# Layer two of a two-layer decoder on one Trainium2 core: gate and up products by Strassen's seven, results through DRAM, down projection chunk by chunk

## The chip, the cores and the metric

The kernel runs on one core of one Trainium2 chip. Its engines work side by side and meet at semaphores: TensorE (PE; its weight loads are PEld), VectorE (DVE), ScalarE (ACT), GpSimd (POOL), and SyncE (SP), whose queue issues all DMAs of the part in question. The metric is the device time in microseconds (us) from start to end of one execution; lower is better.

## The reference, cut to what matters

A decoder trunk on x of 1024 tokens by D = 1024: a convolution layer with a gated feed-forward, then a differential-attention layer with another, then a final RMSNorm. Only the second feed-forward changes:

```
def rmsnorm(x, g):
    x32 = x.astype(jnp.float32)
    y = x32 * lax.rsqrt(jnp.mean(x32 * x32, axis=-1, keepdims=True) + EPS)
    return (y * g.astype(jnp.float32)).astype(x.dtype)
...
def swiglu(h, w1, w3, w2):
    return (jax.nn.silu(h @ w1) * (h @ w3)) @ w2
...
        x = x + swiglu(rmsnorm(x, ffn_norm_g[layer]), ffn_w1[layer], ffn_w3[layer], ffn_w2[layer])
...
    return rmsnorm(x, final_norm_g)
```

All tensors are float32, D_FF = 2816.

## The kernel before, in words

**Numbers.** A float32 product is made of three matmuls: each operand is split into a high part of type fp32r (a copy by ACT, which rounds) and a low part (operand minus high part, by DVE), and PE adds low weight by high data, high weight by low data, high by high (`product`). Names end in h and l for the two parts: `Wh`, `Wl` for weights, `Sh`, `Sl` for the normed input with features on partitions.

**Sizes.** P = 128, KC = D / P = 8 pieces of the contraction, FC = 2816 / 128 = 22 chunks of hidden features, HT = 512 tokens in a half; the halves are LA and LB. A block of weights is 128 x 1024 float32 (512 KB). `load` brings it into one of two buffers `raw` (rows of 512 bytes), ACT's `hi` and DVE's `lo` split it into one of RING = 4 slots, and `raw` is loaded again after `lo` of the block two earlier (`load` waits for `w_lo`).

**Layer two's feed-forward** is the object `F1`. Its 22 chunks come in groups of 6, 6, 6 and 4. For each chunk of a group, a w1 block and a w3 block are multiplied with both halves (`both`, 2 x 24 matmuls of 512 columns a block); DVE scales the results by `rstd` (L1307, L1316), ACT takes the silu, DVE multiplies (L1319) and splits (L1281) them into `G1h`, `G1l` in SBUF. After each of the first three groups, KC blocks of w2 are multiplied with the group's chunks and DVE adds the results to the residual `xT` (L1326). The weight of the last group's w2 (`Th`, `Tl`, `TAIL_SIZE` = 4 chunks) serves three parts of the tokens, `PARTS`, of 512, 256 and 256 tokens. In the last parts PE also turns finished token blocks back (`y_chunks`, 8 transposes of 128 x 128 at L1605 for a block of 128 tokens), ACT sums their squares (L1102), DVE scales (`y_row`, L1590) and SP stores them.

**Order.** All orders are written out by hand, an engine runs its list in order, and a wait holds up everything behind it on its engine.

## Time and profile before

| | |
|---|---|
| median of 3 timed runs | 2398.87 us (2397.82 to 2400.33) |
| the profiled execution, its own time | 2400.49 us |
| its span, first to last instruction | 2398.7 us |
| PE busy | 2340.0 us (98%) |
| DVE busy | 1404.3 us (59%) |
| ACT busy | 800.7 us (33%) |
| mean granted TensorE clock, share of full speed | 0.994 |
| moved by DMA | 154.63 MB, mean 64 GB/s |

The profiled execution's own time lies 1.8 us over its span, and 1.6 us over the median. Matmuls overlap in the profile: the busy time of one is longer than the distance from its start to the next start, so what PE costs is read from distances between starts.

### The profile page before, as it was taken

How to read it: one execution, taken by the hardware profiler on the slowest of the kernel's cores; microseconds unless marked ns; L12 is line 12 of the kernel's file. 1: busy time of each engine (PE TensorE's matmuls, PEld its weight loads, DVE VectorE, ACT ScalarE, POOL GpSimd, SP SyncE). 2: the span in 40 equal slices, each digit the busy share in tenths (PEclk: the TensorE clock that was granted, in tenths of full speed). 3: DMA queues.
4: the chain of work that ended last, by engine and by line, in shares of the span. 5: the costliest groups of instructions: out<-in, count | busy, mean ns of one | idle time of the engine just before them, and what ended most of it. 6: DMA issues, size and time to landing. Idle time of an engine off the chain costs nothing.

```text
span 2398.7 us, 27168 instructions
## 1 busy us (share of the span) xinstructions
PE 2340.0 (98%) x10989; PEld 1899.4 (79%) x10989; DVE 1404.3 (59%) x2145; ACT 800.7 (33%) x1381; POOL 68.2 (3%) x51
## 2 busy tenths in 40 slices
PE   7999989999999999999999999899999999999998
PEld 6875868888788888887777777677888888888888
DVE  6996599999456544446677767656532332233334
ACT  5312432222344322224555555644321111121112
POOL 0000000000000000002111111000000000000000
PEclk9999999999999999999999999999999999999999
DMA  4110323333233333331011111111112111111112
GB/s 137 44 37 17 86 73 96 98 89 96 82 100 92 105 88 97 98 97 52 19 36 49 42 44 48 62 41 36 53 36 62 44 55 51 53 42 46 53 45 80
DMA packets 278010, 154.63 MB, mean 64 GB/s; under 512 B 5669, under 2 KB 273278, under 8 KB 277886
## 3 DMA queue, kind: packets, MB, share of 16 engines
q1 hardware_dynamic: 277886, 152.90, 21.7%
q8 instruction: 88, 1.44, 0.3%
q14 instruction: 36, 0.29, 0.0%
HBM read 145.54 MB, written 7.34 MB: 64 GB/s over the span
## 4 chain that ended last, share of the span: by engine, by line
PE 89%; DVE 7%; ACT 2%; issue 1%; SPq 0%; DMA 0%; DVEq 0%; ACTq 0%
PE ps L1773 28%; PE ps L1622 19%; PE ps L1624 18%; PE ps L1623 18%; PE ps L1605 3%; DVE cacc L1190 2%; DVE cvA L1190 1%; PE ps L1725 1%; DVE sc L1436 1%; ACT sc L964 1%; PE ps L1687 1%; DVE Wl L1115 0%; PE ps L1677 0%; DVE Sl L1351 0%; DVE Wl L1391 0%
## 5 line engine op out<-in xcount | busy, mean ns | idle before, releaser
L1622 PE MATMUL ps<-Sh,Wl 128*128 128x512 f32 x1616 | 656.9, 406 | 20.7 <-DVE Sl L1273 7.4
L1624 PE MATMUL ps<-Sh,Wh 128*128 128x512 f32 x1616 | 632.9, 392 | 0.0
L1623 PE MATMUL ps<-Sl,Wh 128*128 128x512 f32 x1616 | 632.2, 391 | 0.0
L1622 PEld LDWEIGHTS ps<-Sh,Wl 128*128 128x128 f32 x1616 | 305.5, 189 | 99.2 <-issue 27.8
L1624 PEld LDWEIGHTS ps<-Sh,Wh 128*128 128x128 f32 x1616 | 304.7, 189 | 65.8
L1115 DVE TENSOR_TENSOR Wl<-raw,Wh 128x1024 fp32r<-128x1024 f32 (+2 forms) x238 | 280.3, 1178 | 125.2 <-ACT Wh L750 123.5
L1623 PEld LDWEIGHTS ps<-Sl,Wh 128*128 128x128 f32 x1616 | 305.5, 189 | 60.2 <-issue 3.8
L750 ACT ACTIVATE Wh<-raw 128x1024 fp32r<-128x1024 f32 (+2 forms) x238 | 240.8, 1015 | 294.5 <-DMA raw<-in_ffn_w_dram 137.3
L1773 PE MATMUL ps<-Sh,Wl 128*128 128x512 f32 x688 | 213.3, 391 | 2.5 <-DVE Sl L1351 2.4
L1773 PE MATMUL ps<-Sl,Wh 128*128 128x512 f32 x688 | 212.4, 390 | 0.0
L1773 PE MATMUL ps<-Sh,Wh 128*128 128x512 f32 x688 | 212.3, 390 | 0.0
L1326 DVE TENSOR_TENSOR xT<-ps,xT 128x512 f32<-128x512 f32 x96 | 64.0, 688 | 214.7 <-PE ps L1773 133.6
L1773 PEld LDWEIGHTS ps<-Sh,Wl 128*128 128x128 f32 x688 | 129.5, 188 | 30.6 <-issue 3.3
L1773 PEld LDWEIGHTS ps<-Sl,Wh 128*128 128x128 f32 x688 | 129.7, 188 | 26.9
L1773 PEld LDWEIGHTS ps<-Sh,Wh 128*128 128x128 f32 x688 | 129.5, 188 | 27.0
L1316 DVE TENSOR_TENSOR tmp<-ps,rstd 128x512 f32<-128x512 f32 x66 | 45.4, 689 | 167.3 <-PE ps L1773 130.6
L1622 PE MATMUL ps<-G0h,Wl 128*128 128x512 f32 x352 | 138.6, 394 | 0.0
L1624 PE MATMUL ps<-G0h,Wh 128*128 128x512 f32 x352 | 137.0, 389 | 0.0
L1623 PE MATMUL ps<-G0l,Wh 128*128 128x512 f32 x352 | 137.0, 389 | 0.0
L874 ACT ACTIVATE tmp<-tmp 128x512 f32<-128x512 f32 x66 | 41.0, 632 | 262.1 <-DVE tmp L1307 262.1
L1307 DVE TENSOR_TENSOR tmp<-ps,rstd 128x512 f32<-128x512 f32 x66 | 43.5, 687 | 139.7 <-PE ps L1773 116.5
L977 ACT ACTIVATE ATh<-ps 128x512 fp32r<-128x512 f32 (+2 forms) x96 | 47.0, 490 | 202.3 <-PE ps L1605 202.3
(196 smaller groups left out, 3116.5 us busy)
## 6 DMA issues: line engine op xcount, KB each, us to landing
raw<-in_ffn_w_dram SPq DMA_DIRECT2D x148, 512.0 KB, 3.8
raw<-in_pw_w_dram SPq DMA_DIRECT2D x32, 512.0 KB, 3.8
raw<-in_ffn_w_dram SPq DMA_DIRECT2D x32, 448.0 KB, 3.7
raw<-in_ffn_w_dram SPq DMA_DIRECT2D x24, 384.0 KB, 3.4
xrow<-in_x_dram SPq DMA_DIRECT2D x8, 512.0 KB, 6.6
raw<-in_w_q_dram SPq DMA_DIRECT2D x8, 512.0 KB, 4.7
raw<-in_w_k_dram SPq DMA_DIRECT2D x8, 512.0 KB, 4.1
raw<-in_w_v_dram SPq DMA_DIRECT2D x8, 512.0 KB, 3.9
```

What stands on the lines that cost most here:

```text
L750: act.activation(flat(ring_hi(b)), flat(raw[b % 2][:, 0:n, :]), ACT.Copy).then_inc(w_hi, 1)
L977: act.activation(ATh[:, j0:j0 + nj, (i % 2) * P:(i % 2 + 1) * P], ps[:, BANK[key], 0:nj * P].rearrange("p (j q) -> p j q", q=P), ACT.Copy) ...
L1115: dve.tensor_tensor(flat(ring_lo(b)), flat(raw[b % 2][:, 0:n, :]), flat(ring_hi(b)).bitcast(F32), ALU.subtract).then_inc(w_lo, 1)
L1190: dve.scalar_tensor_tensor(dst, src, wj, dst, ALU.mult, ALU.add).then_inc(conv_s, 1)
L1307: dve.tensor_tensor(plain, ps[:, bank, :], rstd[:, hf, :], ALU.mult).then_inc(t1_ok, 1)
L1316: dve.tensor_tensor(gated, ps[:, bank, :], rstd[:, hf, :], ALU.mult).then_inc(t3_ok, 1)
L1326: dve.tensor_tensor(X(c, hf), by_block(ps[:, bank, :]), X(c, hf), ALU.add).then_inc(add_ok, 1)
L1605: return pe.transpose(dst, src, ident[0:m, 0:m])
L1622: pe.matmul(dst, ll, rh, start=start, stop=False)
L1623: pe.matmul(dst, lh, rl, start=False, stop=False)
L1624: return pe.matmul(dst, lh, rh, start=False, stop=stop)
L1773: ins = pe.matmul(ps[:, banks[j], :], (Wh if m else Wl)[s][:, k, :], l if m == 1 else h, start=k == 0 and m == 0, stop=k == chunks - 1 and ...
```

## The change

`F1` keeps one group of four chunks (CHUNKS0), without w2. The other 18 chunks go in pairs; for each pair there is one *unit* for w1 (u even) and one for w3 (u odd), UNITS = 18. A unit takes two chunks by two halves of tokens by two halves of the contraction (HC = 4 pieces) as a 2 x 2 by 2 x 2 product of quarters, in Strassen's way (Winograd's form): PE makes seven products of 4 x 3 matmuls (A11, S2, A12, S1, S3, S4, A22) in place of eight. DVE makes four sums of weight quarters a unit (`weight_sums_first`, `weight_sums_last`), splits seven (`up_low`), and combines the seven results by seven additions from PSUM (`read`), four scalings and, for odd units, four multiplications. The sums of input quarters (T1 to T4) are made once, beside the plain group. `raw[0]` and `raw[1]` hold the two chunks of one unit, and `up_load(u)` fills both after the last `up_low` of the unit before. Products go round through all eight banks of PSUM.

The 44 hidden tiles (22 chunks, 2 halves) are stored to `g_dram`. The down projection takes 22 chunks for each of the three parts, 66 *steps*: a step loads one chunk of w2 for all 1024 outputs (512 KB, rows of 4096 bytes) and the chunk's hidden tile, both are split, and PE adds 8 x 3 matmuls into eight results that stay in PSUM over all 22 steps. So w2 is loaded three times. Turns of finished blocks (`Y_TURN_AT`) follow steps 2, 6, 10 and 14 of part 1 and steps 4 and 9 of part 2; the last two blocks' turns follow the last step.

```
-F1 = Ffn(1, (LA, LB), (6, 6, 6, 4), WO0 + KC + 1, F0B.result0 + F0B.results(), 2 * FC, FC, 6 * KC, False, True)
-
+F1 = Ffn(1, (LA, LB), (4,), WO0 + KC + 1, F0B.result0 + F0B.results(), 2 * FC, FC, 6 * KC, False, True)
...
+CHUNKS0 = F1.sizes[0]
+UNITS = FC - CHUNKS0
+PRODUCTS = 7
+ALL_PRODUCTS = PRODUCTS * UNITS
+USLOTS = 8
+HC = KC // 2
+A11, S2, A12, S1, S3, S4, A22 = range(PRODUCTS)
...
+UBANKS = (6, 7, 4, 5, 0, 1, 2, 3)
...
+DOWN_ORDER = ((2, 3, 6, 7, 4, 5, 0, 1), tuple(range(KC)), tuple(range(KC)))
+DOWN_BANK = (tuple((n, 0) for n in range(KC)), tuple(((2, 3, 6, 7)[n // 2], n % 2 * HT // 2) for n in range(KC)),
+             tuple(((4, 5, 0, 1)[n // 2], n % 2 * HT // 2) for n in range(KC)))
+STEPS_D = len(PARTS) * FC
...
+Y_TURN_AT = {(1, 2): 0, (1, 6): 1, (1, 10): 2, (1, 14): 3, (2, 4): 4, (2, 9): 5}
...
+            def up_load(u):
+                if u:
+                    sp.wait_ge(u_lo, PRODUCTS * u)
+                else:
+                    sp.wait_ge(w_lo, TAIL)
+                for r in range(2):
+                    sp.dma_start(raw[r][:, :, :], cols(up3 if u % 2 else up1, CHUNKS0 + 2 * (u // 2) + r)) \
+                        .then_inc(u_in[r], 16)
...
+            def unit_store(u, j):
+                sp.wait_ge(u_g, 4 * (u // 2) + j + 1)
+                c, hf = tiles(u)[j]
+                sp.dma_start(g_dram[c, hf], st[:, j, :]).then_inc(g_out[j], 16)
+            def down_load(d):
+                if d >= 2:
+                    sp.wait_ge(dw_lo, d - 1)
+                else:
+                    sp.wait_ge(u_lo, ALL_PRODUCTS)
+                sp.dma_start(raw[d % 2][:, :, :], down[d % FC]).then_inc(dw_in[d % 2], 16)
+            def hidden_load(d):
+                if d >= 4:
+                    sp.wait_ge(dg_lo, d - 3)
+                else:
+                    sp.wait_ge(up_mm, ALL_PRODUCTS - PRODUCTS + S2 + 1)
...
+                sp.dma_start(graw[d % 4][:, 0:w], g_dram[k, hf, :, c0:c0 + w]).then_inc(dg_in[d % 4], 16)
...
+            def second_layer():
+                blocks = list(F1.order())
+                for _, what, c, b in blocks[0:4]:
+                    load(b, cols(up1 if what == "w1" else up3, c))
+                for i in range(len(blocks)):
+                    if i + 4 < len(blocks):
+                        _, what, c, b = blocks[i + 4]
+                        load(b, cols(up1 if what == "w1" else up3, c))
+                    if i == 6:
+                        up_load(0)
+                    if i % 2:
+                        hidden_store(i // 2)
+                for u in range(UNITS):
+                    if u + 1 < UNITS:
+                        up_load(u + 1)
+                    else:
+                        down_load(0)
+                        down_load(1)
+                    if u % 2:
+                        for j in range(4):
+                            unit_store(u, j)
+                            if u == UNITS - 1 and j < 2:
+                                hidden_load(2 * j)
+                                hidden_load(2 * j + 1)
+                for j in range(4):
+                    sp.wait_ge(g_out[j], 16 * (UNITS // 2))
+                sp.dma_start(grow[:, :], a["final_norm_g"].unsqueeze(0).broadcast_to([P, D])).then_inc(grow_in, 16)
+                for d in range(2, STEPS_D):
+                    down_load(d)
+                    if d >= 4:
+                        hidden_load(d)
+                    t = y_behind(d - 8)
+                    if t is not None:
+                        y_store(t)
...
+            def up_high(u, j):
+                q = PRODUCTS * u + j
+                if j == A11:
+                    for r in range(2):
+                        act.wait_ge(u_in[r], 16 * (u + 1))
+                if j in (S1, S2, S3, S4):
+                    act.wait_ge(u_sum, 4 * u + (S1, S2, S3, S4).index(j) + 1)
+                if q >= USLOTS:
+                    act.wait_ge(up_mm, q - USLOTS + 1)
+                else:
+                    act.wait_ge(mm, results_through(TAIL - RING + q // 2))
...
+                act.activation(flat(Uh[uslot(q)]), flat(src), ACT.Copy).then_inc(u_hi, 1)
...
+            for u in range(UNITS):
+                act.wait_ge(up_mm, PRODUCTS * u + 1)
+                if u:
+                    act.wait_ge(u_ev, READS * (u - 1) + E_11)
+                else:
+                    act.wait_ge(g_st[LA], 16 * CHUNKS0)
+                act.activation(p1, ps[:, ubank(PRODUCTS * u + A11), :], ACT.Copy).then_inc(p1_ok, 1)
+                for turn, js in enumerate(((A11,), (S2, A12, S1), (S3, S4), (A22,), ())):
+                    if u + 1 < UNITS:
+                        for j in js:
+                            up_high(u + 1, j)
+                    if u % 2 == 0 and turn < 4:
+                        up_silu(u, turn)
...
+            for d in range(STEPS_D):
+                act.wait_ge(dw_in[d % 2], 16 * (d // 2 + 1))
+                if d < RING:
+                    act.wait_ge(up_mm, ALL_PRODUCTS - USLOTS + 2 * d + 2)
+                else:
+                    step_done(act, d - RING)
+                act.activation(flat(Wh[down_slot(d)]), flat(raw[d % 2]), ACT.Copy).then_inc(dw_hi, 1)
...
+                act.activation(Dh[d % 4][:, 0:w], graw[d % 4][:, 0:w], ACT.Copy).then_inc(dg_hi, 1)
+                t = y_behind(d - 3)
+                if t is not None:
+                    y_square(t)
...
+            def up_low(u, j):
...
+                dve.wait_ge(u_hi, q + 1)
+                dve.tensor_tensor(flat(Ul[r]), flat(src), flat(Uh[r]).bitcast(F32), ALU.subtract).then_inc(u_lo, 1)
...
+            def weight_sums_first(u):
+                for r in range(2):
+                    dve.wait_ge(u_in[r], 16 * (u + 1))
+                s1 = up_slot(u, S1)
+                dve.tensor_tensor(s1, raw[1][:, 0:HC, :], raw[1][:, HC:KC, :], ALU.add).then_inc(u_sum, 1)
+                dve.wait_ge(u_sum, 4 * u + 1)
+                dve.tensor_tensor(s2v[:, :, :], s1, raw[0][:, 0:HC, :], ALU.subtract).then_inc(u_sum, 1)
+            def weight_sums_last(u):
+                s3 = up_slot(u, S3)
+                dve.tensor_tensor(s3, raw[0][:, 0:HC, :], raw[1][:, 0:HC, :], ALU.subtract).then_inc(u_sum, 1)
+                dve.wait_ge(u_sum, 4 * u + 2)
+                s4 = up_slot(u, S4)
+                dve.tensor_tensor(s4, raw[0][:, HC:KC, :], s2v[:, :, :], ALU.subtract).then_inc(u_sum, 1)
...
+            def read(u, j, reads, to, other):
+                dve.wait_ge(up_mm, PRODUCTS * u + j + 1)
+                dve.tensor_tensor(to, ps[:, ubank(PRODUCTS * u + j), :], other, ALU.add).then_inc(u_ev, 1)
+                dve.wait_ge(u_ev, READS * u + reads)
+            def result_of(u, i, j, reads, other, hf):
+                c0 = u // 2
+                to = va if u % 2 else st[:, i, :]
+                if u % 2 == 0 and c0:
+                    dve.wait_ge(g_out[i], 16 * c0)
+                elif u % 2 and 4 * c0 + i:
+                    dve.wait_ge(u_g, 4 * c0 + i)
+                read(u, j, reads, to, other)
+                dve.tensor_tensor(to, to, rstd[:, hf, :], ALU.mult).then_inc(u_t, 1)
+                if u % 2:
+                    dve.wait_ge(u_t, 4 * u + i + 1)
+                    dve.wait_ge(u_silu, 4 * c0 + i + 1)
+                    dve.tensor_tensor(st[:, i, :], to, st[:, i, :], ALU.mult).then_inc(u_g, 1)
+            ffn(F1, beside_f1)
+            sum_low(0, 3)
+            up_low(0, A22)
+            dve.wait_ge(t_lo, 4 * HC)
+            for hf in F1.halves:
+                dve.wait_ge(g_st[hf], 16 * CHUNKS0)
+            for u in range(UNITS):
+                more = u + 1 < UNITS
+                dve.wait_ge(p1_ok, u + 1)
+                read(u, S2, E_Q6, q6, p1)
+                result_of(u, 0, A12, E_11, p1, LA)
+                if more:
+                    weight_sums_first(u + 1)
+                    up_low(u + 1, A11)
+                read(u, S1, E_U4, u4, q6)
+                if more:
+                    up_low(u + 1, S2)
+                    up_low(u + 1, A12)
+                    up_low(u + 1, S1)
+                result_of(u, 1, S3, E_22, u4, LB)
+                read(u, S3, E_U3, q6, q6)
+                if more:
+                    weight_sums_last(u + 1)
+                result_of(u, 2, S4, E_12, u4, LB)
+                if more:
+                    up_low(u + 1, S3)
+                    up_low(u + 1, S4)
+                result_of(u, 3, A22, E_21, q6, LA)
+                if more:
+                    up_low(u + 1, A22)
...
+            for d in range(STEPS_D):
+                dve.wait_ge(dw_hi, d + 1)
+                dve.tensor_tensor(flat(Wl[down_slot(d)]), flat(raw[d % 2]), flat(Wh[down_slot(d)]).bitcast(F32),
+                                  ALU.subtract).then_inc(dw_lo, 1)
+                w = PARTS[d // FC][1]
+                dve.wait_ge(dg_hi, d + 1)
+                dve.tensor_tensor(Dl[d % 4][:, 0:w], graw[d % 4][:, 0:w], Dh[d % 4][:, 0:w].bitcast(F32),
+                                  ALU.subtract).then_inc(dg_lo, 1)
+                if d % FC == 2 and d > FC:
+                    down_adds(d // FC - 1)
+                t = y_behind(d - 3)
+                if t is not None:
+                    if t == 0:
+                        dve.wait_ge(grow_in, 16)
+                    y_row(t)
...
+            def product_read(q):
+                u, j = q // PRODUCTS, q % PRODUCTS
+                if j == A11:
+                    pe.wait_ge(p1_ok, u + 1)
+                else:
+                    pe.wait_ge(u_ev, READS * u + last_read[j])
+            def up_product(u, j):
+                q = PRODUCTS * u + j
+                pe.wait_ge(u_lo, q + 1)
+                if u == 0 and j in sums_of:
+                    pe.wait_ge(t_lo, HC * sums_of[j])
+                if q >= len(UBANKS):
+                    product_read(q - len(UBANKS))
...
+                h, l = quarters[j]
+                r = uslot(q)
+                for k in range(HC):
+                    ins = product(ps[:, ubank(q), :], Uh[r][:, k, :], Ul[r][:, k, :], h[:, k, :], l[:, k, :], k == 0,
+                                  k == HC - 1)
+                ins.then_inc(up_mm, 1)
+            for u in range(UNITS):
+                for j in range(PRODUCTS):
+                    up_product(u, j)
...
+            for d in range(STEPS_D):
+                part, k = d // FC, d % FC
+                w = PARTS[part][1]
+                pe.wait_ge(dw_lo, d + 1)
+                pe.wait_ge(dg_lo, d + 1)
+                r = down_slot(d)
+                for n in DOWN_ORDER[part]:
+                    bank, c0 = DOWN_BANK[part][n]
+                    if k == 0:
+                        down_free(part, n)
+                    ins = product(ps[:, bank, c0:c0 + w], Wh[r][:, n, :], Wl[r][:, n, :], Dh[d % 4][:, 0:w],
+                                  Dl[d % 4][:, 0:w], k == 0 and c0 == 0, k == FC - 1 and c0 + w == HT)
+                    if k == FC - 1:
+                        ins.then_inc(d_res, 1)
+                if k < FC - 1:
+                    ins.then_inc(d_step, 1)
+                t = y_behind(d)
+                if t is not None:
+                    y_chunks(t, range(KC))```

**PE, in a unit.** The rows are matmuls (moving and stationary operand named; `Uh`, `Ul` are the slots of weight quarters, T3 the input sum for S3). Before, a w1 block:

```order
L1773 MATMUL ps<-Sh,Wl_111 128x512 [waits add_ok,w_lo]
```

Of the change, the first row of five products that follow one another, without the eleven of each between them:

```order
L1979 MATMUL ps<-T3h,Ul_94 128x512 [waits u_ev,u_lo]
...
L1979 MATMUL ps<-Sh,Ul_95 128x512 [waits u_ev,u_lo]
...
L1979 MATMUL ps<-T4h,Ul_96 128x512 [waits u_ev,u_lo]
...
L1979 MATMUL ps<-Sh,Ul_89 128x512 [waits u_ev,u_lo]
...
L1979 MATMUL ps<-T2h,Ul_90 128x512 [waits p1_ok,u_lo]
```

A block waited once for 48 matmuls; a product waits for 12, for its weight quarter (`u_lo`) and for its bank (`u_ev`, `p1_ok`).

**DVE, from a w1 unit into a w3 unit.** Before, a w1 and a w3 block had this list (two results scaled, a block's low part, two results scaled and multiplied, the hidden low parts):

```order
L1307 TENSOR_TENSOR tmp_73<-ps,rstd 128x512 [waits mm] x2
L1115 TENSOR_TENSOR Wl_110<-raw_104,Wh_106 128x1024 [waits w_hi]
L1316 TENSOR_TENSOR tmp_73<-ps,rstd 128x512 [waits mm]
L1319 TENSOR_TENSOR tmp_73<-tmp_73 128x512 [waits silu_ok,t3_ok]
L1316 TENSOR_TENSOR tmp_73<-ps,rstd 128x512 [waits mm]
L1319 TENSOR_TENSOR tmp_73<-tmp_73 128x512 [waits silu_ok,t3_ok]
L1281 TENSOR_TENSOR G1l<-tmp_73,G1h 128x512 [waits hid_hi] x2
```

Now, from the last `up_low` of one unit to the sums and low parts of the next:

```order
L1827 TENSOR_TENSOR Ul_96<-raw_139,Uh_88 128x512 [waits u_hi]
L1873 TENSOR_TENSOR q_107<-ps,p_106 128x512 [waits up_mm,p1_ok]
L1873 TENSOR_TENSOR va<-ps,p_106 128x512 [waits up_mm,u_ev]
L1885 TENSOR_TENSOR va<-va,rstd 128x512 [waits u_ev]
L1889 TENSOR_TENSOR st<-va,st 128x512 [waits u_silu,u_t]
L1842 TENSOR_TENSOR Us_100<-raw_139 128x512 [waits up_mm,u_in1,u_in0]
L1844 TENSOR_TENSOR s2v<-Us_100,raw_138 128x512 [waits u_sum]
L1827 TENSOR_TENSOR Ul_89<-raw_138,Uh_81 128x512 [waits u_hi]
L1873 TENSOR_TENSOR u_108<-ps,q_107 128x512 [waits up_mm]
L1827 TENSOR_TENSOR Ul_90<-s2v,Uh_82 128x512 [waits u_hi,u_ev]
L1827 TENSOR_TENSOR Ul_91<-raw_138,Uh_83 128x512 [waits u_hi]
L1827 TENSOR_TENSOR Ul_92<-Us_100,Uh_84 128x512 [waits u_hi]
```

Between the first row, which frees `raw` (its last reader), and L1842, which waits for both new chunks (`u_in0`, `u_in1`), stand four operations of w3 units and three of w1 units; the rest of the unit stands behind L1842.

**SP, in units and in steps.** Before, each load waited for the low part two blocks earlier:

```order
L565 DMA raw_104<-in_ffn_w_dram 128x8x128 [waits w_lo]
L565 DMA raw_105<-in_ffn_w_dram 128x6x128 [waits w_lo]
```

Now two units, with the four stores of a w3 unit, and further on two steps of part 1:

```order
L681 DMA raw_138<-in_ffn_w_dram 128x8x128 [waits u_lo]
L681 DMA raw_139<-in_ffn_w_dram 128x8x128
L693 DMA g_dram<-st 128x512 [waits u_g] x4
L681 DMA raw_138<-in_ffn_w_dram 128x8x128 [waits u_lo]
L681 DMA raw_139<-in_ffn_w_dram 128x8x128
...
L700 DMA raw_139<-in_ffn_w_dram 128x1024 [waits dw_lo]
L714 DMA graw_114<-g_dram 128x256 [waits g_out1,dg_lo]
L700 DMA raw_138<-in_ffn_w_dram 128x1024 [waits dw_lo]
L714 DMA graw_111<-g_dram 128x256 [waits g_out2,dg_lo]
```

Both chunks of a unit are now asked for at once, behind the stores where there are any, and every step has a second load behind that of w2.

## Rows read from the trace of the kernel before

**Rows 1.** The page: span, and busy time of the engines.

```profile
span 2398.7 us, 27168 instructions
PE 2340.0 (98%) x10989; PEld 1899.4 (79%) x10989; DVE 1404.3 (59%) x2145; ACT 800.7 (33%) x1381; POOL 68.2 (3%) x51
```

**Rows 2.** Busy time by stretch: layer two's feed-forward; its columns first.

```profile
core 0: us, PE busy (x) PEld busy (x) DVE busy (x) ACT busy (x) POOL busy (x), PEclk, DMA share, GB/s
1661.00:2339.00 678.00, 677.90 (x2979) 560.26 (x2979) 244.31 (x322) 137.68 (x191) 0.00 (x0) 1.00 0.17 49
```

**Rows 3.** The chain that ended last: start, us, engine, line, count.

```profile
1686.45 642.06 PE ps L1773 x2832
```

**Rows 4.** Timeline of PE in the tail: start, us, engine, line, operation.

```profile
2361.10 0.28 PE L1623 MATMUL ps<-G1l,Th 128*128 128x256 f32 x1
...
2362.30 0.28 PE L1624 MATMUL ps<-G1h,Th 128*128 128x256 f32 x1
2362.42 1.04 PE L1605 MATMUL ps<-ident,xT 128*128 128x128 f32 x8
2363.22 0.36 PE L1622 MATMUL ps<-G1h,Tl 128*128 128x256 f32 x1
```

**Rows 5.** Timeline of DVE: operations of 512 columns, chained and unchained.

```profile
1655.26 3.85 DVE L1477 TENSOR_TENSOR xT<-ps,xT 128x512 f32<-128x512 f32 x6
...
1659.90 10.69 DVE L1351 SCALAR_TENSOR_TENSOR Sl<-xT,vec,Sh 128x512 fp32r<-128x512 f32 x16 [0.79 <-ACT Sh L1089]
...
1708.17 0.69 DVE L1316 TENSOR_TENSOR tmp<-ps,rstd 128x512 f32<-128x512 f32 x1 [1.46 <-PE ps L1773]
1708.89 0.69 DVE L1319 TENSOR_TENSOR tmp<-tmp 128x512 f32<-128x512 f32 x1
1709.50 0.68 DVE L1316 TENSOR_TENSOR tmp<-ps,rstd 128x512 f32<-128x512 f32 x1
```

**Rows 6.** Tile raw from 1661 to 2300 us: min/median/max ns, then landing.

```profile
L750 ACT ACTIVATE Wh<-raw x65: 828/1043/1061, 1669.0 to 2299.0; 128x1024 fp32r<-128x1024 f32 x41, 128x768 fp32r<-128x768 f32 x24
L1115 DVE TENSOR_TENSOR Wl<-raw,Wh x64: 948/1216/1226, 1670.5 to 2287.7; 128x1024 fp32r<-128x1024 f32 x40, 128x768 fp32r<-128x768 f32 x24
DMA to landing us min/median/max: 3.2/3.7/4.6
```

**Rows 7.** The page's DMA issues: count, KB each, median us to landing.

```profile
raw<-in_w_q_dram SPq DMA_DIRECT2D x8, 512.0 KB, 4.7
...
raw<-in_w_o_dram SPq DMA_DIRECT2D x1, 512.0 KB, 3.6
```

**Rows 8.** Line L565 from 1649 to 1651 us: two loads overlapping, to landing.

```profile
L565 SPq DMA_DIRECT2D raw<-in_ffn_w_dram x2: 367/368/368, 1649.4 to 1650.6; - x2
...
DMA to landing us min/median/max: 3.8/4.4/5.1
```

**Rows 9.** Timeline of PE: two starts with the idle time before them.

```profile
1552.85 0.79 PE L1622 MATMUL ps<-Sh,Wl 128*128 128x512 f32 x1 [4.70 <-DVE Wl L1391]
...
1660.80 1.37 PE L1773 MATMUL ps<-Sh,Wl 128*128 128x512 f32 x2 [2.42 <-DVE Sl L1351]
```

**Rows 10.** Stretches after the two idle times; columns as in rows 2.

```profile
1552.00:1554.00 2.00, 1.15 (x3) 0.96 (x4) 1.93 (x5) 0.00 (x0) 0.00 (x0) 0.50 0.01 3
1556.00:1558.00 2.00, 2.00 (x10) 1.90 (x10) 0.07 (x1) 0.35 (x1) 0.00 (x0) 0.50 0.05 8
...
1662.00:1664.00 2.00, 2.00 (x6) 1.61 (x5) 2.00 (x4) 2.00 (x4) 0.00 (x0) 0.50 0.03 8
```

**Rows 11.** Timeline of the end: last matmuls, last addition, last scaling.

```profile
2390.16 0.28 PE L1624 MATMUL ps<-G1h,Th 128*128 128x256 f32 x1
2390.28 1.12 PE L1605 MATMUL ps<-ident,xT 128*128 128x128 f32 x6
2390.48 0.42 DVE L1583 TENSOR_TENSOR xT<-ps,xT 128x256 f32<-128x256 f32 x1 [2.10 <-PE ps L1624]
...
2391.32 1.02 ACT L1102 ACTIVATE sq<-ps 128x1024 f32<-128x1024 f32 x1 [9.12 <-PE ps L1605]
```

334 lines of the change are left out of this document (220 added, 114 removed).

## The prediction, made before the changed kernel ran

> **What bounds the kernel now.** I read the page first. PE is busy for 2340.0 of 2398.7 us, DVE for 59%, ACT for 33% [rows 1]. Such a busy share overstates PE, since matmuls overlap in it, so I took the stretch of layer two's feed-forward next: PE is busy for 677.90 of its 678.00 us [rows 2]. The chain of work that ended last says the same, and gives the price: 2832 matmuls of 512 columns in 642.06 us [rows 3], 0.2267 us each, start to start. PE waits for nothing there. The tail has the other price: eleven starts of 256-column matmuls from 2361.10 to 2362.30 us [rows 4], 0.120 us each, so two narrow ones cost 0.013 us more than a wide one. Every matmul less is a gain of 0.2267 us, as long as nothing else becomes late. The reader should therefore look at the other engines and the loads in the new order.
>
> **PE's own work.** Up and gate: a unit of eight products of 12 matmuls becomes seven. 18 units x 12 = 216 wide matmuls fewer: -49.0 us. A unit is now 84 x 0.2267 = 19.04 us. Down: before, 960 wide and 192 narrow ones; now 22 x 24 = 528 wide and 44 x 24 = 1056 narrow ones: -432 x 0.2267 + 864 x 0.120 = +5.7 us. Together -43.2 us.
>
> **The unit as a loop of loads.** This is the term I looked at longest. `raw` is freed by the last `up_low` of a unit; only then are both next chunks asked for, and DVE needs both before its first sum. What stands behind the sum must be done before `raw` is free again. So a unit lasts at least load + DVE's work behind the sum, whatever PE does.
> DVE's price: a multiplication that needs the one before it starts 0.72 us after it (1708.17 to 1708.89), the next, which needs nothing, 0.61 us later [rows 5]. Six additions in a row take 3.85 us and 16 splits that wait for ACT 10.69 us, thus 0.63 and 0.66 us apiece [rows 5]. I take 0.65 us for free ones and 0.72 us for chained ones. Behind the sum a w1 unit has 19 operations, 6 of them chained: 12.8 us. A w3 unit has three more multiplications and three more chained places: 15.0 us. Mean 13.9 us.
> The load's price: one block lands after 3.7 us [rows 6]. Two blocks asked for 1.2 us apart, at 1649.4 and 1650.6 us, landed after 3.8 and 5.1 us [rows 8], so both were there 6.3 us after the first was issued. Issued 0.37 us apart (the issue itself takes 0.367 us), two should take between 5.5 us (3.7 + 1.8, the second hidden to a half) and 6.3 us. I take 5.8, and 0.2 us for the stores in front of every second pair.
> Loop: 13.9 + 6.0 = 19.9 us against PE's 19.04: late by 0.86 us a unit. PE feels it only when the lead is gone. The last split for unit 0 ends some 4.9 us into the unit (two scalings, four splits of T1 and one more after the plain group's last matmul). PE needs the next unit's first split at 19.04 us, and it comes at lag + 6.0 + 2.1 us; so the lag may grow to about 11. Growing by 0.86 a unit, and with the early odd unit held by its product rather than its load, it gets there around unit 8; nine units remain: 9 x 0.86 = +8 us. Bounds: at 0.61 us an operation and 5.5 us a load the loop is 18.8 us, nothing is lost; at 0.72 us throughout and 6.3 us it is 21.1 us, +28 us. ACT is no bound: at most eleven copies and silus a unit at 0.6 us. PSUM is none: a product needs the bank of eight products ago, read over half a unit earlier.
>
> **From units to steps.** The last result must be read, scaled and multiplied (2.2 us at 0.72), then DVE splits the first w2 chunk (1.22 us [rows 6]) and the first tile (0.69 us [rows 5]). Both stand behind it in DVE's list. With a wake-up of PE that is 4.2 us idle; the trace has no cover for it. Then comes the clock. After 4.70 us idle PE ran at 0.50, 1.2 GHz, in stretches from 1552 to 1558 us, and after 2.42 us idle again at 0.50 in 1662 to 1664 us [rows 9, 10]. At half the clock 6 us lose 3 us and 3.4 us lose 1.7; I take 2.4. Term: +6.6 us (5.5 to 8).
> The Trainium skill's "TensorE: Matmul & The Clock Gate", Part 1, speaks against this place of the change: an idle array drops to half its clock and needs sustained work to come back. The trace agrees (0.50 in rows 10); by a sum without the rule the term would be 4.2 us.
>
> **The steps of the down projection.** A wide step is 24 x 0.2267 = 5.4 us, a narrow one 24 x 0.120 = 2.88 us. A buffer `raw` goes round in landing + ACT's copy + DVE's split: 3.7 + 1.04 + 1.22 us [rows 6] + 0.2 for hand-overs = 6.2 us, and there are two: 3.1 us a step. The one load with rows of 4 KB landed after 3.6 us [rows 7]; the hidden tile's load behind each shares the queue, so I take 6.4 us, 3.2 a step. Wide steps hide that. Over 44 narrow steps the supply falls behind by 0.32 us each, 14 us; against it stand six turns, which stop PE for 0.80 us each [rows 4] but not the loads, and a reserve of some 6 us (up to three split chunks ahead, reduced by DVE's additions between parts). +3 us; bounds 0 and, with a landing of 4.7 us as for w_q [rows 7], 44 x 0.70 - 11 = +20.
> Bandwidth is no bound: 640 KB in 3.2 us; the mean of 49 GB/s [rows 2] rises to some 200, and SP has 0.37 + 0.34 us of issuing in a step.
>
> **Hidden at nothing.** The input sums (16 operations, about 10 us of DVE beside blocks of 48 x 0.2267 = 10.9 us, with DVE busy for 244 of 678 us [rows 2]), the stores of the plain tiles, and the load for the final gain (before the third chunk's load; that chunk is needed 11 us later). If the last cover is gone, it costs its 5 us once.
> **End.** The last eight additions now fall on the last step; two remain after it (0.42 us each [rows 11]) instead of one, and 16 transposes wait for them; one interruption of PE by early transposes goes away. 0, within 1.5 us.
>
> **Sum.** -43.2 + 8 + 6.6 + 3 = -25.6 us on the profiled execution's 2400.5: 2374.9; that execution lies 1.6 us over the median of the timed runs, so 2373 us.
>
> **Rivals.**
> (A) Forecast: units end up limited by the load loop, late and mildly. 2367 to 2381 us. 42%.
> (B) The loop stays under PE or never uses up its lead: the two loads land within 4.9 us of issue, or DVE's free operations run at 0.61 (loop 19.4 us, lag short of 11). Then units cost 19.04 us each and the time is 2373 - 8 = 2365, with no step stalls 2362. For it: 0.61 and 0.63 in rows 5. Against: 6.3 us in rows 8. 25%.
> The Trainium skill's "DMA: Bandwidth & Descriptors" (Anatomy of one DMA) gives 2.0 us plus size over 436 GB/s, an estimate of 4.4 us for the pair, which is this rival's case; the 3.7 us that this trace has for half of it is over the page's 3.2.
> (C) The change doesn't do what it says: the loop is so long that seven products last as long as eight (21.8 us). From 20.6 us on, more than half is eaten. At 21.1 us: 2373 + 20 = 2393; range 2382 to 2402. For it: up to 26 operations in a unit, nearly each behind a wait of its own. 15%.
> (D) Narrow steps wait for their loads: at 4.7 us to landing, 2373 + 17 = 2390. 10%.
> (E) The other side, slower than before: the same place, decided by one number. From a landing of 5.1 us on (3.78 us a step, 44 x 0.90 - 11 = 28.6 us) the gain is gone, from 5.3 us on it is slower by more than 0.2%; at 6 us it would be 2415. What speaks for it is that each step's 512 KB has a second load ahead of it in the queue; against, that no block of this layer took over 4.6 us [rows 6]. 5%. Some 3% is for what I don't see, such as a hold-up in the plain group.
>
> **Numbers.** The likeliest is A: 2373. Leaving out the upper part of C and of D, and E, and the lowest edge of B, the range is 2361 to 2389. 0.2% (4.8 us) is about what the measurement can tell from no change. Faster by more: A, B, D and most of C: 0.91. Within: 0.03. Slower: 0.06.
>
> **What would show it.** Right: starts 0.227 and 0.120 us apart in the new lines; a unit of 19.0 us first and 19.9 us later, with PE's wait before the first product of a unit and DVE's longest wait at L1842 for `raw`; 4 us idle and a clock of 0.50 before the first step; narrow steps of 2.9 us early and 3.2 us late in a part. Wrong: PE waiting for PSUM (`u_ev`) in a unit, units over 20.6 us, landings of w2 over 4.7 us, or DVE operations over 0.72 us apart.

## The result, and the profile after

The changed kernel takes 2371.23 us (median of 4 runs, 2370.46 to 2373.89). The kernel before, run beside it, takes 2399.6 us (median of 4, 2397.82 to 2401.53). The ratio is 0.9884, with a 95% interval from 0.9866 to 0.9901: 28 us faster. The profiled executions stand 29.3 us apart in their spans (2398.7 and 2369.4).

The page of the kernel after, the lines that answer to [rows 1], and the count of DMA packets:

```profile
span 2369.4 us, 28710 instructions
PE 2302.7 (97%) x11205; PEld 1884.7 (80%) x11205; DVE 1609.1 (68%) x2473; ACT 904.2 (38%) x1569; POOL 67.4 (3%) x51
DMA packets 280324, 200.88 MB, mean 85 GB/s; under 512 B 7973, under 2 KB 258686, under 8 KB 280190
```

Busy time by stretch of the kernel after, with the columns of [rows 2]: the units, the first w2 step, the other wide steps, the first part of narrow steps, the second part.

```profile
1742.00:2093.00 351.00, 351.00 (x1550) 290.66 (x1549) 280.56 (x436) 108.26 (x188) 0.00 (x0) 1.00 0.28 83
2098.60:2105.40 6.80, 6.80 (x18) 5.36 (x19) 1.61 (x2) 0.61 (x1) 0.00 (x0) 0.57 0.66 231
2105.00:2221.00 116.00, 116.00 (x513) 96.03 (x512) 43.55 (x51) 35.38 (x46) 0.00 (x0) 1.00 0.45 149
2221.00:2289.50 68.50, 67.47 (x562) 66.92 (x560) 39.01 (x52) 33.67 (x53) 0.00 (x0) 1.00 0.68 216
2289.50:2360.00 70.50, 66.79 (x544) 65.50 (x544) 39.99 (x60) 31.49 (x48) 0.00 (x0) 1.00 0.63 203
```

PE is busy through all of the units, although DVE is now busy for 281 of 351 us. It is not fully busy in the two parts of narrow steps, 1.0 and 3.7 us short. The granted clock is 1.00 but for the first step (0.57). The timeline of PE in the kernel after: the start of unit 0, of unit 16 and of unit 17, then the last matmul of the units and the first of the down projection.

```profile
1751.25 0.39 PE L1979 MATMUL ps<-Sh,Ul 128*128 128x512 f32 x1
...
2055.89 0.39 PE L1979 MATMUL ps<-Sh,Ul 128*128 128x512 f32 x1
...
2074.93 0.39 PE L1979 MATMUL ps<-Sh,Ul 128*128 128x512 f32 x1
...
2093.75 0.39 PE L1981 MATMUL ps<-T4h,Uh 128*128 128x512 f32 x1
2098.58 0.76 PE L1979 MATMUL ps<-Dh,Wl 128*128 128x512 f32 x1 [4.44 <-DVE Wl L1942]
```

From unit 0 to unit 17 there are 323.68 us, and 323.68 / 17 = 19.04 us is PE's own time for a unit: it waited in none. Whether the load loop is longer shows in when DVE gets its first sum for the next unit. The timeline of DVE in the kernel after, that sum in unit 0 and in unit 16:

```profile
1761.71 0.69 DVE L1842 TENSOR_TENSOR Us<-raw 128x512 f32<-128x512 f32 x1 [0.61 <-DMA raw<-in_ffn_w_dram]
...
2072.28 0.69 DVE L1842 TENSOR_TENSOR Us<-raw 128x512 f32<-128x512 f32 x1 [3.68 <-DMA raw<-in_ffn_w_dram]
```

The sum stands 10.46 us behind its unit's start at first (1761.71 - 1751.25) and 16.39 us sixteen units later (2072.28 - 2055.89): it slips by 0.37 us a unit. So the loop takes 19.04 + 0.37 = 19.41 us, longer than PE's 19.04, as forecast, but with less slip. By the forecast's 2.1 us from this sum to the first split, PE would begin to wait when the sum comes 19.04 - 2.1 = 16.9 us behind its unit's start. The last unit came 0.5 us before that.

The change of phase, the timeline of DVE in the kernel after:

```profile
2094.59 0.69 DVE L1873 TENSOR_TENSOR va<-ps,q 128x512 f32<-128x512 f32 x1 [0.83 <-PE ps L1981]
2095.32 0.69 DVE L1885 TENSOR_TENSOR va<-va,rstd 128x512 f32<-128x512 f32 x1
2096.05 0.69 DVE L1889 TENSOR_TENSOR st<-va,st 128x512 f32<-128x512 f32 x1
2096.66 1.22 DVE L1942 TENSOR_TENSOR Wl<-raw,Wh 128x1024 fp32r<-128x1024 f32 x1
2097.79 0.68 DVE L1946 TENSOR_TENSOR Dl<-graw,Dh 128x512 fp32r<-128x512 f32 x1
```

It is the forecast's list, in its order: result, two multiplications, chunk, tile. From the end of PE's work (2093.75 + 0.23) to its next start are 4.6 us. The first step then lasts 8.29 us instead of 5.44 (the loss of the half clock, 2.85 us; in the six experiments that keep the pause it is 1.7 to 2.9 us). Together 7.5 us.

The narrow steps, the waits of PE and of its weight loads from 2110 to 2361 us in the kernel after (total us, times, longest), one from each of two answers:

```profile
PE ps L1979 <- DVE Dl L1946: 4.4, 6, 1.1
...
PEld ps L1979 <- DVE Wl L1942: 6.0, 7, 1.2
```

Weight loads wait ahead of time, so these don't add up. From the starts of the steps, with 2.88 us for a narrow step and 0.80 us for a turn, the 44 steps hold 7.5 us too much; 0.4 of it is there as well in kernels in which PE never waits, so 7.1 us are waits. The first wait is at 2277 us, and SP's timeline ten us earlier shows where it begins (start, duration, queue, line):

```profile
2267.71 0.33 SPq L700 DMA_DIRECT2D raw<-in_ffn_w_dram  x1
2268.15 0.38 SPq L714 DMA_DIRECT2D graw<-g_dram  x1
2268.86 0.34 SPq L753 DMA_DIRECT2D out_dram<-yout  x1
```

The chain that ended last, in the kernel after (start, us, what), takes up that load: 6.72 us in place of 3.6, then ACT's copy and DVE's split. From there it goes on to the next load into the same buffer (2276.80); PE starts at 2277.25.

```profile
2267.71 6.72 DMA raw<-in_ffn_w_dram
...
2274.45 1.07 ACT Wh L1319
...
2275.54 1.24 DVE Wl L1942
```

1.15 us after the load a store of a finished output block (L753, 512 KB) was issued. This is the load for step 40, and the load for step 39 had been issued only 1.6 us before it. Two loads as close as that without a store (for steps 30 and 31, 1.47 us apart) cost the second 1.3 us (4.92 us to landing), so the store's share here is nearer 2 us than 3, an estimate from these two landings.

The two longest waits come later, at steps 57 and 62, and each has a store in front of the load that is late. The first of them in PE's timeline:

```profile
2331.90 0.36 PE L1979 MATMUL ps<-Dh,Wl 128*128 128x256 f32 x1 [1.07 <-DVE Dl L1946]
```

The load for step 57 was issued at 2323.22 us, 1.67 us behind a store, and landed after 5.85 us; that for step 62 was issued 1.51 us behind a store and landed after 5.76 us. One wait has another cause: 0.8 us at step 47, whose split stands behind DVE's eight additions between the two parts.

Term by term, from the profiled executions. The last matmul of the down projection starts at 2360.00 and the span ends 9.38 us later; in [rows 11] it was 8.5 us.

| term | forecast | measured |
|---|---|---|
| PE's own work | -43.2 | -43.2 |
| units wait for the load loop | +8 | 0 |
| units to steps | +6.6 | +7.5 |
| narrow steps | +3 | +7.1 |
| end | 0 | +0.8 |
| sum | -25.6 | -27.8 |

The remaining 1.5 us up to the spans' -29.3 lie ahead of the change. At the start of layer two's feed-forward PE pauses for 2.42 us in both kernels. Behind that pause the kernel before ran at 0.50 [rows 9, 10]; the kernel after stayed at full clock, as the row of PE at the end of the pause and the stretch behind it show:

```profile
1661.86 1.07 PE L2127 MATMUL ps<-Sh,Wl 128*128 128x512 f32 x2 [2.42 <-DVE Sl L1572]
1662.00:1664.00 2.00, 1.90 (x8) 1.31 (x9) 2.00 (x4) 2.00 (x5) 0.00 (x0) 1.00 0.00 0
```

Seventeen matmuls from there take 5.87 us before and 4.36 us after. The change has no part in that: of the twelve kernels profiled for this document, all with this pause of 2.42 us, four fell to half clock behind it and eight did not. So 27.8 us of the profiled 29.3 belong to the change.

### The profile page after: what moved, and what is told of

It reads as the page before. It is cut to its first block, busy times and chain, and to the rows that moved or that the text cites. A ratio compares the mean times of both kernels' runs of the same rounds, so it can differ in the third digit from the quotient of the medians.

```text
span 2369.4 us, 28710 instructions
## 1 busy us (share of the span) xinstructions
PE 2302.7 (97%) x11205; PEld 1884.7 (80%) x11205; DVE 1609.1 (68%) x2473; ACT 904.2 (38%) x1569; POOL 67.4 (3%) x51
## 2 busy tenths in 40 slices
DMA packets 280324, 200.88 MB, mean 85 GB/s; under 512 B 7973, under 2 KB 258686, under 8 KB 280190
## 3 DMA queue, kind: packets, MB, share of 16 engines
q1 hardware_dynamic: 280190, 199.04, 27.7%
## 4 chain that ended last, share of the span: by engine, by line
PE 84%; DVE 8%; DMA 3%; ACT 3%; issue 1%; SPq 0%; DVEq 0%; ACTq 0%
PE ps L1979 26%; PE ps L1981 25%; PE ps L1980 25%; PE ps L2127 3%; PE ps L1962 3%; DMA raw<-in_ffn_w_dram 3%; DVE cacc L1414 2%; DVE cvA L1414 2%; PE ps L2082 1%; DVE Wl L1942 1%; DVE sc L1657 1%; ACT sc L1108 1%; ACT Wh L1319 1%; PE ps L2044 1%; DVE Wl L1339 0%
## 5 line engine op out<-in xcount | busy, mean ns | idle before, releaser
L1979 PE MATMUL ps<-Sh,Wl 128*128 128x512 f32 x1616 | 657.5, 407 | 20.1 <-DVE Sl L1497 6.8
L1981 PE MATMUL ps<-Sh,Wh 128*128 128x512 f32 x1616 | 633.3, 392 | 0.0
L1980 PE MATMUL ps<-Sl,Wh 128*128 128x512 f32 x1616 | 632.3, 391 | 0.0
L1979 PEld LDWEIGHTS ps<-Sh,Wl 128*128 128x128 f32 x1616 | 305.4, 189 | 98.6 <-issue 28.2
L1981 PEld LDWEIGHTS ps<-Sh,Wh 128*128 128x128 f32 x1616 | 304.8, 189 | 66.0
L1339 DVE TENSOR_TENSOR Wl<-raw,Wh 128x1024 fp32r<-128x1024 f32 (+1 forms) x178 | 213.3, 1199 | 92.4 <-ACT Wh L898 91.0
L898 ACT ACTIVATE Wh<-raw 128x1024 fp32r<-128x1024 f32 (+1 forms) x178 | 183.2, 1032 | 155.4 <-DMA raw<-in_ffn_w_dram 127.7
L1979 PE MATMUL ps<-Dh,Wl 128*128 128x256 f32 (+1 forms) x528 | 170.7, 323 | 9.2 <-DVE Wl L1942 4.8
L1942 DVE TENSOR_TENSOR Wl<-raw,Wh 128x1024 fp32r<-128x1024 f32 x66 | 80.8, 1224 | 131.3 <-ACT Wh L1319 131.2
L1980 PE MATMUL ps<-Dl,Wh 128*128 128x256 f32 (+1 forms) x528 | 169.0, 320 | 0.0
L1981 PE MATMUL ps<-Dh,Wh 128*128 128x256 f32 (+1 forms) x528 | 168.9, 320 | 0.0
L1979 PE MATMUL ps<-G0h,Wl 128*128 128x512 f32 x352 | 138.6, 394 | 0.0
L1981 PE MATMUL ps<-G0h,Wh 128*128 128x512 f32 x352 | 137.0, 389 | 0.0
L1319 ACT ACTIVATE Wh<-raw 128x1024 fp32r<-128x1024 f32 x66 | 69.9, 1058 | 160.9 <-DMA raw<-in_ffn_w_dram 83.0
L1979 PEld LDWEIGHTS ps<-Dh,Wl 128*128 128x128 f32 x528 | 101.0, 191 | 18.4 <-DVE Wl L1942 10.8
L1979 PE MATMUL ps<-Sh,Ul 128*128 128x512 f32 x288 | 112.0, 389 | 0.0
L1981 PE MATMUL ps<-Sh,Uh 128*128 128x512 f32 x288 | 112.0, 389 | 0.0
## 6 DMA issues: line engine op xcount, KB each, us to landing
raw<-in_ffn_w_dram SPq DMA_DIRECT2D x214, 512.0 KB, 3.9
raw<-in_pw_w_dram SPq DMA_DIRECT2D x32, 512.0 KB, 4.0
xrow<-in_x_dram SPq DMA_DIRECT2D x8, 512.0 KB, 6.3
raw<-in_w_q_dram SPq DMA_DIRECT2D x8, 512.0 KB, 4.7
```

The source lines that it names most:

```text
L898: act.activation(flat(ring_hi(b)), flat(raw[b % 2][:, 0:n, :]), ACT.Copy).then_inc(w_hi, 1)
L1319: act.activation(flat(Wh[down_slot(d)]), flat(raw[d % 2]), ACT.Copy).then_inc(dw_hi, 1)
L1339: dve.tensor_tensor(flat(ring_lo(b)), flat(raw[b % 2][:, 0:n, :]), flat(ring_hi(b)).bitcast(F32), ALU.subtract).then_inc(w_lo, 1)
L1942: dve.tensor_tensor(flat(Wl[down_slot(d)]), flat(raw[d % 2]), flat(Wh[down_slot(d)]).bitcast(F32), ALU.subtract).then_inc(dw_lo, 1)
L1979: pe.matmul(dst, ll, rh, start=start, stop=False)
L1980: pe.matmul(dst, lh, rl, start=False, stop=False)
```

## The experiments

In every result with a range the time is the median of four or five runs; the results without one (the extra product, both kernels with two more operations, the first with the stores last) are single runs. "Against before" is the ratio to the kernel before on the same chip. The wait in the narrow steps is always what the 44 steps take over the 132 us of the kernel that never waits.

**What a product costs, and whether the loop is hidden.** In `up_product` one of the seven products is made twice; PE gets back the eighth product and nothing else changes.

```diff
                 r = uslot(q)
+                for k in range(HC if j == A22 else 0):
+                    product(ps[:, ubank(q), :], Uh[r][:, k, :], Ul[r][:, k, :], h[:, k, :], l[:, k, :], k == 0,
+                            k == HC - 1)
                 for k in range(HC):
```

> Every unit makes its last product (A22) twice into the same bank, so PE has eight products again and everything else is as in the changed kernel; the result is not altered. Theory 1 (PE sets the pace of the units, a wide matmul costs 0.2267 us): 18 x 12 x 0.2267 = +49.0 us, 2420 us; units start 21.76 us apart and DVE's first sum no longer slips against the unit. Rival (units are held by loads and DVE, so the eighth product is hidden in part): well under +49, about +40 if the loop were already as long as the prediction had it.

Measured: 2415.27 us, 44.0 over the change. The units are 21.76 us apart, all of them, and from the first matmul of the units to the last there are 391.45 us instead of 342.49, 48.96 more: 18 x 12 x 0.2267 = 49.0. (The last one comes 49.29 us later, because the first already came 0.33 later.) So in the units the price is exact, and no hidden stall was taken back. The missing 5 us are nearly all in the narrow steps, where PE waited 2.5 us instead of 7.1, with nothing changed there. These waits differ from one execution to the next; the part behind DVE's additions, at step 47, is there in every profiled kernel with two buffers and the stores in their old place (0.8 to 1.2 us).

**How near the load loop is.** Two more DVE operations, chained, behind the sum of each unit, where the forecast puts the lag.

```diff
                     up_low(u + 1, S4)
+                    for n in range(2):
+                        dve.tensor_tensor(u4, q6, q6, ALU.max).then_inc(more_ok, 1)
+                        dve.wait_ge(more_ok, 2 * u + n + 1)
```

> Two more DVE operations of 512 columns, chained, in each of 17 units, behind the first sum and ahead of the split that frees the buffers (their result is not used). Theory 1 (the load loop of load plus DVE work behind the sum is 19.4 us against PE's 19.04, and a lead of some 6 us was just not used up): the loop becomes 19.4 + 1.44 = 20.85 us, the lead is gone after three or four units, 17 x 1.8 - 6.4 = +24 us, 2395 us, with PE waiting before the first product of the later units. Rival (DVE has slack and only its busy time counts, two thirds in this stretch): within 1 us of 2371.

Measured: 2391.51 us, 20.3 over. The first units start 19.04 us apart, then the lead is gone and they take 20.8 us on average. In unit 4 the first sum comes 17.2 us behind the unit's start and the next unit is the first to start late, by 0.2 us, so the limit of 16.9 us holds. The timeline of PE in this kernel, the last product of a unit and the first of the next:

```profile
1885.47 0.39 PE L1985 MATMUL ps<-T4h,Uh 128*128 128x512 f32 x1
1889.10 0.80 PE L1983 MATMUL ps<-Sh,Ul 128*128 128x512 f32 x1 [3.25 <-DVE Ul L1828]
```

And DVE's longest group of waits in it is the forecast's:

```profile
DVE Us L1843 <- DMA raw<-in_ffn_w_dram: 52.2, 17, 5.1
```

So the loop is real. The units alone take 23.5 us more (365.99 us for 342.49), where 24 were expected; an earlier start of the units (1.0 us) and 2.8 us less waiting in the narrow steps make 20 of it. Some 1.4 us of DVE work a unit, 7%, cost that much. The rival, that the units have room to spare, fell.

**The same, with the first chunk asked for early.** The two operations stay; the next first chunk is asked for as soon as the sums have read its buffer, only the second after the last split.

```diff
                 if u:
-                    sp.wait_ge(u_lo, PRODUCTS * u)
+                    sp.wait_ge(u_sum, 4 * u)
...
                 for r in range(2):
+                    if r and u:
+                        sp.wait_ge(u_lo, PRODUCTS * u)
```

> As the kernel with two more DVE operations a unit, but the first of a unit's two chunks is asked for when the last weight sum is made, some 5 us before the second. Theory 1 (the loop of load and DVE's work behind the sum holds those units): only one load, about 4 us, is left in the loop: 13.4 + 1.4 + 4.1 = 18.9 us, under PE's 19.04; PE's waits between units go, 2371 us within 3. Rival (the extra DVE work itself holds them): 2388 us or more, as without the split load.

Measured: 2377.53 us, 14 us back of the 20. That is less than the theory wanted, and the timeline of DVE says why: the first sum before a w3 unit and before a w1 unit.

```profile
1979.15 0.69 DVE L1845 TENSOR_TENSOR Us<-raw 128x512 f32<-128x512 f32 x1 [0.54 <-DMA raw<-in_ffn_w_dram]
...
2001.11 0.69 DVE L1845 TENSOR_TENSOR Us<-raw 128x512 f32<-128x512 f32 x1 [4.00 <-DMA raw<-in_ffn_w_dram]
```

The first wait is short, the second isn't. In every second unit the early request stands in SP's queue behind the four stores of results, the last of which waits for result 4. SP's timeline in this kernel shows both loads issued directly behind that store, as before the edit:

```profile
1994.48 0.32 SPq L696 DMA_DIRECT2D g_dram<-st  x1
1994.84 1.19 SPq L684 DMA_DIRECT2D raw<-in_ffn_w_dram  x2
```

Two units then take (3.9 + 15.9) + (6.0 + 13.7) = 39.5 us (load, then DVE's work behind the sum), and in the trace they are 39.3 to 39.7 us apart.

**Four buffers for the w2 chunks.** Two more 4 KB buffers, in space that is free by then; `down_load` waits for the split four steps back.

```diff
-                if d >= 2:
-                    sp.wait_ge(dw_lo, d - 1)
+                if d >= 4:
+                    sp.wait_ge(dw_lo, d - 3)
+                elif d >= 2:
+                    sp.wait_ge(up_mm, ALL_PRODUCTS)
...
-                sp.dma_start(raw[d % 2][:, :, :], down[d % FC]).then_inc(dw_in[d % 2], 16)
+                sp.dma_start(wraw[d % 4][:, :, :], down[d % FC]).then_inc(dw_in[d % 4], 16)
```

> w2's chunks land in four buffers in turn in place of two, in space that is free after the last unit. Theory 1 (the 6.1 us that PE waits in narrow steps come from two buffers that each take landing + copy + split to go round): the waits go, -6 us, 2365 us. Rival a (the waits come from the time a load takes when out's blocks are stored, or from bandwidth: 640 KB a step): they stay for a good part, -3 us or less. Rival b (DVE's and ACT's own lists at the additions and rows): they stay, within 1 us of 2371.

Measured: 2363.46 us (2361.62 to 2364.3), 0.9851 [0.9836, 0.9865] against before: about 8 us under the change. PE waits for nothing in the narrow steps. So all 7 us go with two more buffers, those behind DVE's additions included.

**Stores at the end.** Two buffers as in the change; all stores of output blocks are issued after the last load.

```diff
-                    t = y_behind(d - 8)
-                    if t is not None:
-                        y_store(t)
...
-            for t in range(TB - 2, TB):
+            for t in range(TB):
```

> The six finished blocks of the output are stored after the last step instead of between the loads of the narrow steps; all else as in the changed kernel. Theory 1 (two buffers going round are the cause, and stores between them make single loads late): PE's waits in narrow steps fall from 7 us to 1 to 4 us, since the loads without a store beside them still take 3.6 us; the stores at the end add 5 to 8 us, so the time is 2372 to 2377 us. Rival (the stores are the whole cause): no wait left in the narrow steps. Other rival (they have no part): the waits stay at 6 to 8 us.

Measured: 2364.29 us, no wait in the narrow steps, and the end as long as before: the rival's case, and the 5 to 8 us for stores at the end were wrong. Once more, with more runs:

> The changed kernel with only the six stores moved behind the last step, as in the one look before, now timed. If the one look (2364.3 us, no waits in the narrow steps) was typical: 2363 to 2366 us, 6 to 7 us under the changed kernel. If landings vary from run to run so much that the one look was lucky: 2367 us or more.

Measured: 2363.87 us (2362.89 to 2364.9), 0.9854 [0.9841, 0.9867], 7.4 us under the change; its profiled execution has 2.3 us of waits in the narrow steps. 1.2 of these are at the very last step: the six stores are now issued 0.85 us behind the last load, which landed after 4.8 us. The other 1.1 us have no store near them, so two buffers alone only just keep up. Landing of the w2 loads from 2221 to 2350 us, in the kernel after:

```profile
DMA to landing us min/median/max: 3.5/3.8/6.7
```

The same with the stores last, in the first of the two runs:

```profile
DMA to landing us min/median/max: 3.4/3.6/4.8
```

And with four buffers:

```profile
DMA to landing us min/median/max: 3.5/4.6/6.3
```

Without stores between them the longest landing falls by 1.9 us and the waits with it. With four buffers the loads land later than in the change, and nobody waits. At the end six stores in a row fit beside the last steps and the final scaling: the last matmul of the down projection starts 9.38 us before the end in both kernels.

**The first step's splits before the last result.** In the last unit, DVE's two splits for step 0 go ahead of result 4, and the first tile is asked for before the unit's stores.

```diff
                 if more:
                     weight_sums_last(u + 1)
+                else:
+                    step_low(0)
                 result_of(u, 2, S4, E_12, u4, LB)
...
+                    if u == UNITS - 1:
+                        hidden_load(0)
                     if u % 2:
```

> DVE splits the first w2 chunk and the first hidden tile before it reads product S4 of the last unit, not after the last result; the first hidden tile is loaded a little earlier for it. Theory 1 (the 4.6 us idle and the 2.9 us at half clock behind it come only from this order in DVE's list): PE goes on within 0.5 us, the clock stays at full, -7.4 us, 2364 us. Rival (the idle time is set by the load of the hidden tile or by the bank of the last product): the first step starts 2 us or more after the last product and the clock still falls, -2 us or less.

Measured: 2369.24 us (2368.08 to 2370.4), 0.9876 [0.986, 0.9893]: 2 us, not 7. PE passes from units to steps without a pause, and stops 11 us later. The timeline of PE in this kernel, before step 2:

```profile
2103.86 0.39 PE L1991 MATMUL ps<-Dh,Wh 128*128 128x512 f32 x1
2107.35 0.77 PE L1989 MATMUL ps<-Dh,Wl 128*128 128x512 f32 x1 [3.10 <-DVE Dl L1901]
```

3.3 us idle, and half clock behind it again. SP's timeline shows what came late: the load of chunk 2 was behind the last two stores of the units and the gain.

```profile
2094.52 2.50 SPq L693 DMA_DIRECT2D g_dram<-st  x2
2098.79 0.33 SPq L745 DMA_DIRECT2D grow<-in_final_norm_g_dram  x1
2099.17 7.79 SPq L700 DMA_DIRECT2D raw<-in_ffn_w_dram  x3
```

In the change step 2 starts only at 2112.3 us, behind the pause and the half clock, and the chunk is there by then.

**The same, with SP's queue in the order of need.** Chunk 2 goes ahead of the last unit store; the gain and its waits go to step 8.

```diff
                         for j in range(4):
+                            if u == UNITS - 1 and j == 3:
+                                down_load(2)
                             unit_store(u, j)
...
-                for d in range(2, STEPS_D):
+                for d in range(3, STEPS_D):
+                    if d == 8:
+                        for j in range(4):
+                            sp.wait_ge(g_out[j], 16 * (UNITS // 2))
```

> The early split, and the load of the third w2 chunk moved ahead of the last hidden store, the final gain's load moved behind that of the eighth chunk. Two buffers as in the changed kernel. Theory 1 (the early split only moved the idle time to step 2, whose chunk stood behind SP's wait for the last stores and the gain's load): no idle time over 1 us and no half clock between the last product and step 3, 2371.2 - 7.4 = 2364 us. Rival (another cause behind step 2's wait, such as DVE's list): an idle time of 2 us or more stays in the first steps and the time stays at 2367 us or over.

Measured: 2363.81 us (2361.24 to 2364.84), 0.985 [0.9837, 0.9863], 7.4 us under the change, as forecast. Busy time in the two stretches around the change of phase, columns as in [rows 2]:

```profile
2092.00:2099.00 7.00, 7.00 (x32) 5.53 (x31) 6.50 (x10) 0.43 (x2) 0.00 (x0) 1.00 0.66 221
2099.00:2106.00 7.00, 7.00 (x32) 5.78 (x32) 3.74 (x5) 4.13 (x6) 0.00 (x0) 1.00 0.71 218
```

PE is busy throughout and the granted clock stays at 1.00, 2.4 GHz. With the pause the half clock is gone too.

**Everything together.** Early splits, SP's order (with four buffers the load of chunk 3 goes ahead of the last unit store too), four buffers:

> Four buffers, early split and the new order of loads together. If the two costs are apart in time, their gains add: 2363.5 - 7.4 = 2356 us. If not (bandwidth or DVE is short once PE goes on at once), 2360 us or more.

Measured: 2356.24 us (2353.99 to 2357.72), 0.9822 [0.9809, 0.9836]. Early splits, SP's order, two buffers and the stores last:

> Two buffers, early split, new order of loads, and the six finished blocks stored after the last step. Theory 1 (the stores between the loads are the whole cause of the waits in narrow steps, and the two buffers alone keep up): no wait over 0.3 us in the narrow steps, no idle time at the first step, 2356 us, the same as with four buffers. Rival (two buffers keep up only by luck of one run): 2 us or more of waits come back, 2358 to 2362 us.

Measured: 2356.48 us (2354.42 to 2358.24), 0.9822 [0.9808, 0.9835], with 1.7 us of waits in its last ten steps, the longest 0.6 us and not under 0.3 as expected. Busy time in the narrow steps of the first of the two:

```profile
2211.00:2343.00 132.00, 132.00 (x1107) 131.96 (x1106) 78.34 (x112) 65.03 (x101) 0.00 (x0) 1.00 0.64 210
```

PE is busy for all 132.00 us. These are the fastest versions: 43 us under the kernel before and 15 under the change. 43.2 us is what PE's own work was to give: no wait of PE in units or steps eats into it any more. (That the two agree to 0.2 us is chance, with 0.8 us more at the end and a half clock ahead of the units that comes and goes.)

## Why the prediction was right, and where it was not

**The time.** 2373 forecast, 2371.2 measured, in the likeliest case's 2367 to 2381. That it is so close is luck: two large errors of opposite sign, 8 us too much in the units and 4 too little in the narrow steps, nearly cancel with the small ones (0.9 us at the change of phase, 0.8 at the end, and 1.5 us of a half clock ahead of the change, which no sum could foresee). What case A forecast for the units, PE held up by the load loop, did not happen; rival B (25%), whose time was 2365, had the units right.

**PE's own work**, -43.2: right. The doubled product (48.96 us for 49.0) shows the unit's share; the two best versions show the whole.

**The load loop**, +8: the loop is there, but it took nothing from PE. The failed value is "I take 0.65 us for free ones". It lies between 0.63 and 0.66 us, and the 0.66 came from splits that wait for ACT; the 0.61 of a free operation stood beside them. In the kernel after, free operations follow each other at 0.61 us, and what stands behind the sum takes 12.3 us (w1) and 14.5 us (w3) instead of 12.8 and 15.0. The load's 6.0 us were right (mean of 5.7 to 6.9 from the first issue to DVE's first sum). The loop is 19.4 us, rival B's figure, and the slip 0.37 instead of 0.86 us a unit. Over 16 units that is 5.9 us, and the lead held some 6.4: the case nearest to the edge. Two operations more and the term is there, with 20 us.
The two loads issued together had both landed after 5.6 to 6.8 us. The estimate of 4.4 us from the Trainium skill's "DMA: Bandwidth & Descriptors" (Anatomy of one DMA) was too low for this pair, and with it the loop would have been shorter than PE's unit; the trace does not bear that out. The Trainium skill gives that formula for DMAs issued from GpSimd, and these loads are issued by SyncE.

**Units to steps**, +6.6: right in place, order and size (7.5). That it can be had back is shown, by the early splits together with SP's order; that by itself the first does not bring it is shown too. Of the 7.5 us 2.9 are the clock: the granted clock is 0.57 on average from 2098.60 to 2105.40, after 4.6 us of idle time, and 1.00 at the same place when PE doesn't pause. The rule of the Trainium skill's "TensorE: Matmul & The Clock Gate" (Part 1), that an idle array falls to its lower clock, agrees with both. Behind the shorter pause of 2.42 us the prediction's reading (0.50 in [rows 10]) is one of two outcomes: the kernel after stayed at 1.00 there.

**Narrow steps**, +3: too low, 7.1. The step that failed is the supply's: "the hidden tile's load behind each shares the queue, so I take 6.4 us" counts the loads and leaves out the stores of finished output blocks, 512 KB each, that share the DMA engines with them. A load beside one landed after up to 6.7 us instead of 3.6; the 15 loads of w2 that had a store under way beside them took 3.5 to 6.7 us, median 4.2, the 19 that had neither a store nor another load of w2 3.4 to 4.4, median 3.6. Rival D had the place right (narrow steps wait for their loads); its cause, a constant landing of 4.7 us, was not there, the median is 3.8. With the stores moved the waits were 0 and 2.3 us and the time fell by 7.4 us, and with buffers added the waits were gone; that makes the stores' part shown. DVE's eight additions, which the prediction has only as a cut in the reserve, stand behind 0.8 us of the waits. Open is how much a load loses for each store: the waits of kernels that are alike in this stretch ran from 2.5 to 7.1 us, each from one profiled execution.

**End**, 0 within 1.5: 0.8, right. **The covers** held: PE had no wait in the plain group or for PSUM. The gain's load did cost nothing in the change, but only because the pause covered it; that cover was gone in the kernel with early splits alone.

## What to carry to other kernels

A loop of loads that is longer than the engine it feeds costs nothing until its lead is used up: compare slip per round times rounds with the lead, since here 0.37 us a round against 0.86 decided over 8 us. When a stall at a change of phase is removed, read the issuing queue for what is due next, because a load behind a store inherits the store's wait; here the stall came back two steps later until the queue was put in the order of need. Where loads have just enough buffers, keep large stores out of that stretch or give the loads more buffers: each of the two alone gave 7 to 8 us. Four buffers left no wait in either kernel that has them; with the stores moved and two buffers 0 to 2.3 us were left.
